# Retention and mLSTM head outputs kept with queries as rows instead of channels as rows

## The reference

```python
proj = x @ w_in[l]                 # split into r_q r_k r_v r_g, m_qk, m_v, m_o, m_i, m_f, g_a, g_b
o_ret = _head_norm(_retention(rq, rk, rv), ret_norm_g[l]) * silu(r_g)
o_ml  = _head_norm(_mlstm(mq, mk, mv, i_pre, f_pre), mlstm_norm_g[l]) * sigmoid(m_o)
mix = (sigmoid(g_a + ba) * (o_ret @ w_proj_ret[l]) + sigmoid(g_b + bb) * (o_ml @ w_proj_mlstm[l])) @ w_out[l]
x = _layer_norm(alpha * x + mix, ...);  x = _layer_norm(alpha * x + swiglu(x), ...)
```

## Time and profile before

| | before |
|---|---|
| time, median of 3 runs | 2080.57 us (2076.99 to 2081.15) |
| profiled execution, its own time | 2082.32 us |
| its span in the trace | 2080.2 us |
| PE busy in the span | 98% |
| DVE / ACT / POOL busy | 61% / 48% / 4% |
| mean granted TensorE clock | 0.993 |

### The profile page before, as it was taken

How to read it: one execution, slowest core, us unless ns; L and a number is a source line. 1 busy time by engine, 2 the same in 40 slices (tenths; PEclk the granted TensorE clock), 3 DMA queues, 4 the chain that set the end, 5 groups by cost and what they waited for, 6 DMA issues and landing times.

```text
span 2080.2 us, 37327 instructions
## 1 busy us (share of the span) xinstructions
PE 2047.2 (98%) x15913; PEld 1959.2 (94%) x15928; DVE 1271.8 (61%) x1141; ACT 999.4 (48%) x929; POOL 86.8 (4%) x58
## 2 busy tenths in 40 slices
PE   9999999999999999899999999999999999999998
PEld 8999998999999998589999999999998999999997
DVE  6556655755665576637555665676446674676545
ACT  5545645543454356435344663544344554544333
POOL 2000000100000001101000000100000000100000
PEclk9999999999999999999999999999999999999999
DMA  7555453455555544125554434464554544464552
GB/s 297 182 181 182 166 178 118 161 188 181 181 203 182 192 179 174 61 87 206 181 187 179 164 141 163 176 243 166 183 192 157 197 142 142 167 228 183 192 181 102
DMA packets 51217, 362.31 MB, mean 174 GB/s; under 512 B 5680, under 2 KB 6832, under 8 KB 7728
## 3 DMA queue, kind: packets, MB, share of 16 engines
q1 hardware_dynamic: 49856, 353.05, 47.4%
q0 software_dynamic: 1264, 7.80, 1.1%
HBM read 359.78 MB, written 1.05 MB: 173 GB/s over the span
## 4 chain that ended last, share of the span: by engine, by line
PE 92%; DVE 3%; ACT 2%; DMA 1%; issue 1%; POOL 0%; DVEq 0%; SPq 0%; ACTq 0%; POOLq 0%
PE ps L242 22%; PE ps L243 22%; PE ps L244 22%; PE ps L518 3%; PE ps L519 3%; PE ps L517 3%; PE ps L289 2%; PE ps L290 2%; PE ps L291 2%; PE ps L501 1%; PE ps L495 1%; PE ps L496 1%; DMA raw<-in_slots 1%; PE ps L789 1%; PE ps L1619 1%
## 5 line engine op out<-in xcount | busy, mean ns | idle before, releaser
L238 DVE TENSOR_TENSOR wlo<-raw,whi 128x2048 fp32r<-128x2048 f32 x325 | 758.9, 2337 | 476.4 <-ACT whi L233 475.6
L242 PE MATMUL ps<-in_hi,whi 128*128 128x256 f32 x3596 | 1016.7, 283 | 3.8 <-DVE in_lo L313 3.5
L243 PE MATMUL ps<-in_lo,whi 128*128 128x256 f32 x3596 | 1006.5, 280 | 0.0
L244 PE MATMUL ps<-in_hi,wlo 128*128 128x256 f32 x3596 | 1005.3, 280 | 0.0
L233 ACT ACTIVATE whi<-raw 128x2048 fp32r<-128x2048 f32 x325 | 619.4, 1908 | 214.8 <-PE ps L244 184.4
L242 PEld LDWEIGHTS ps<-in_hi,whi 128*128 128x128 f32 x3596 | 678.6, 189 | 12.3 <-DVE in_lo L313 4.7
L243 PEld LDWEIGHTS ps<-in_lo,whi 128*128 128x128 f32 x3596 | 678.7, 189 | 3.5 <-issue 1.7
L244 PEld LDWEIGHTS ps<-in_hi,wlo 128*128 128x128 f32 x3596 | 678.4, 189 | 0.0
L242 PE MATMUL ps<-h_hi,whi 128*128 128x256 f32 x480 | 134.5, 280 | 0.0
L243 PE MATMUL ps<-h_lo,whi 128*128 128x256 f32 x480 | 133.9, 279 | 0.0
L244 PE MATMUL ps<-h_hi,wlo 128*128 128x256 f32 x480 | 133.9, 279 | 0.0
(11 more groups left out here) (295 smaller groups left out, 2162.9 us busy)
## 6 DMA issues: line engine op xcount, KB each, us to landing
raw<-in_slots SPq DMA_DIRECT2D x333, 1024.0 KB, 4.8
ws<-in_lngb POOLq DMA_DIRECT2D x4, 1024.0 KB, 5.1
ws<-in_mem_t POOLq DMA_DIRECT2D x2, 1024.0 KB, 10.1
consts<-in_consts SPq DMA_DIRECT2D x1, 1600.0 KB, 14.6
consts<-in_consts POOLq DMA_DIRECT2D x1, 1472.0 KB, 6.7
x<-in_x_t SPq DMA_DIRECT2D x1, 1024.0 KB, 7.9
y<-x SPq DMA_DIRECT2D x1, 512.0 KB, 2.6
y<-x SPq DMA_DIRECT2D x2, 256.0 KB, 2.1
```

The source lines that it names most:

```text
L238: dve.tensor_tensor(wlo[:, j], raw[:, j], whi[:, j].bitcast(F32), ALU.subtract).then_inc(lo_ready, 1)
L242: pe.matmul(out, whi[:, j, o:o + n], hi, start=start, stop=False, skip_group_check=True)
L243: pe.matmul(out, whi[:, j, o:o + n], lo, start=False, stop=False, skip_group_check=True)
L244: return pe.matmul(out, wlo[:, j, o:o + n], hi, start=False, stop=stop, skip_group_check=True)
```

## The change

The scores are now the stationary operand and the values are streamed, so the outputs of both mixers have queries as rows and the 256 channels of a head along the free axis. `pe_values2` makes 12 products of 256 columns per mixer. Mean and variance come from DVE's BN_STATS and BN_AGGR straight from PSUM, factor and shift are 128 x 8 numbers, and ACT applies them while it copies PSUM to SBUF (`act_head_norm`, 8 activations of 256 columns). For mLSTM the sum `den` is now a one-column product behind each value product with the same stationary scores; the reciprocal is 128 x 8 numbers and is folded into factor and shift. exp(-m) is turned together with the row `a` (4 tiny products in place of 2), so that L1797's spread has only the running maximum: 256 columns in place of 512. The eight output-gate slots 17 to 24 are made in the tok form, and each gate is one DVE multiplication of 128 x 2048. The result is turned back by 16 TensorE transposes per mixer (`pe_head_turn`), for retention between slots 30 and 31, for mLSTM between slots 33 and 34. The gain of each channel is applied while the turned result is split (`act_head_hi`, `dve_head_lo`, per 256 columns from PSUM). POOL's additions, ACT's squares and all of `pe_head_sums` are gone.

```diff
         def pe_values2(pe, v, sums=None):
+            def both(t, h, w, first, done, tk):
+                last = pe.matmul(head_out(t, h), w, v[:, tk, h * 256:(h + 1) * 256], start=first, stop=done, ...)
+                if sums is not None:
+                    last = pe.matmul(sums(t, h), w, ones[:, 0:1], start=first, stop=done, skip_group_check=True)
+                return last
             for h in range(HEADS):
-                for d in range(2):
-                    o = ps[:, h, d * T:(d + 1) * T]
-                    w = slice(h * 256 + d * P, h * 256 + (d + 1) * P)
-                    pe.matmul(o, v[:, 0, w], scores2[:, h, P:384], start=True, stop=False, ...)
-                    last = pe.matmul(o[:, P:T], v[:, 1, w], scores2[:, h, 0:P], start=False, stop=True, ...)
+                both(0, h, scores2[:, h, P:2 * P], True, True, 0)
+                both(1, h, scores2[:, h, 2 * P:384], True, False, 0)
+                last = both(1, h, scores2[:, h, 0:P], False, True, 1)
...
+        def act_head_norm(act, n, out):
+            act.wait_ge(hn_shift, 2 * n + 2)
+            for t in range(2):
+                for h in range(HEADS):
+                    g = 4 * t + h
+                    last = act.activation(out[:, t, h * 256:(h + 1) * 256], head_out(t, h), ACT.Identity,
+                                          scale=hn_scale[:, g:g + 1], bias=hn_bias[:, g:g + 1])
+            last.then_inc(hn_done, 1)
...
+        def pe_head_turn(pe, n, src):
+            for k in range(DT):
+                for t in range(2):
+                    last = pe.transpose(head_turned(n, k)[:, t * P:(t + 1) * P], src[:, t, k * P:(k + 1) * P], ident)
+                if k % 4 == 3:
+                    last.then_inc(hn_turned, 1)
...
-            run(S_MQK + 1, S_MQK + 3)
-            pe_head_sums(pe, n, "mean")
-            run(S_MQK + 3, S_MV)
-            run(S_MV, S_MV + 2, True)
-            pe_head_sums(pe, n, "var")
-            run(S_MV + 2, S_RG, True)
-            pe.wait_ge(cen_act, CA("factor", n))
+            run(S_MQK + 1, S_MV)
+            run(S_MV, S_RG, True)
+            pe.wait_ge(hn_done, n + 1)
             for h in range(HEADS):
-                last = pe.matmul(ps[:, h, :], const("sel")[0:4, h * P:(h + 1) * P],
-                                 rows[0:4, ROW_M:ROW_E + 1, :].rearrange("p a b -> p (a b)"), start=True, stop=True)
+                last = pe.matmul(ps[:, h, 0:T], const("sel")[0:4, h * P:(h + 1) * P], rows[0:4, ROW_M, :],
+                                 start=True, stop=True)
...
-            run(S_RG + 3, S_MO)
+            run(S_RG + 3, S_MO + 1, True)
             pe.wait_ge(ml_dve, LD("scores", l))
-            for h in range(HEADS):
-                pe.matmul(den[:, h], ones, scores2[:, h, P:384], start=True, stop=False, skip_group_check=True)
-                last = pe.matmul(den[:, h, P:T], ones, scores2[:, h, 0:P], start=False, stop=True, ...)
-            run(S_MO, S_MO + 2)
-            pe.wait_ge(ml_dve, LD("denom", l))
-            pe_values2(pe, l_v).then_inc(ml_pe, 1)
-            run(S_MO + 2, S_GA + 3)
-            pe_head_sums(pe, n + 1, "mean")
-            run(S_GA + 3, S_GB + 2)
-            pe_head_sums(pe, n + 1, "var")
+            pe_values2(pe, l_v, lambda t, h: den[:, 4 * t + h:4 * t + h + 1]).then_inc(ml_pe, 1)
+            run(S_MO + 1, S_GA, True)
+            run(S_GA, S_GB + 2)
+            pe.wait_ge(ret_dve, TD("gated", l))
+            pe.wait_ge(hn_done, n + 2)
+            pe_head_turn(pe, n, r_o)
```

More of the change, by code:

```diff
@@ L1639, in pe_head_sums @@
-        def pe_head_sums(pe, n, step):
-            out = head_mean if step == "mean" else head_var
-            pe.wait_ge(cen_pool, CP(step, n))
-            for h in range(HEADS):
-                last = pe.matmul(out[:, h], ones, c_sq[:, 2 * h], start=True, stop=True, skip_group_check=True)
-            last.then_inc(cen_pe, 1)
-        def dve_head_centre(dve, n, src):
-            dve.wait_ge(cen_pe, CP("mean", n))
-            for h in range(HEADS):
-                v = src[:, 2 * h:2 * h + 2]
-                last = dve.scalar_tensor_tensor(v, bcast(head_mean[:, h], 2), -1.0 / 256, v, ALU.mult, ALU.add)
-            last.then_inc(cen_dve, 1)
@@ L1672, in build, with dve_head_lo @@
+        def dve_head_lo(dve, n, sp, gain, k0, m, at):
+            dve.wait_ge(split_hi, sp + 1)
+            for k in range(k0, k0 + m):
+                last = dve.scalar_tensor_tensor(in_lo[:, at + k - k0], head_turned(n, k), gain(k),
+                                                in_hi[:, at + k - k0].bitcast(F32), ALU.mult, ALU.subtract)
+            last.then_inc(split_lo, 1)
         LN_SUMS = 12
@@ L1783, in layer2_pe @@
             pe.wait_ge(ml_act, LA("en", l))
-            for t in range(2):
-                last = pe.matmul(ps[:, 7, 256 + 4 * t:260 + 4 * t], rows[0:4, ROW_A, t * P:(t + 1) * P], ident[0:4, 0:4],
-                                 start=True, stop=True, skip_group_check=True)
-            last.then_inc(ml_pe, 1)
-            run(S_MQK + 1, S_MQK + 3)
-            pe_head_sums(pe, n, "mean")
-            run(S_MQK + 3, S_MV)
-            run(S_MV, S_MV + 2, True)
-            pe_head_sums(pe, n, "var")
@@ L1793, in layer2_pe @@
-            run(S_MV + 2, S_RG, True)
-            pe.wait_ge(cen_act, CA("factor", n))
+            for i, row in enumerate((ROW_A, ROW_E)):
+                for t in range(2):
+                    o = 256 + 8 * i + 4 * t
+                    last = pe.matmul(ps[:, 7, o:o + 4], rows[0:4, row, t * P:(t + 1) * P], ident[0:4, 0:4],
+                                     start=True, stop=True, skip_group_check=True)
+            last.then_inc(ml_pe, 1)
+            run(S_MQK + 1, S_MV)
+            run(S_MV, S_RG, True)
@@ L2138, in layer2_dve @@
[L2138 to L2144 removed]
+            dve.reciprocal(l_rd[:, :], l_rd[:, :]).then_inc(ml_dve, 1)
+            dve.wait_ge(ml_dve, LD("recip", l))
```

238 lines of the change are left out of this document (121 added, 117 removed).

## The result

| | before | changed |
|---|---|---|
| median, four executions each on one chip | 2080.86 us (2076.99 to 2081.43) | 2067.86 us (2063.28 to 2070.20) |
| profiled execution, its own time / span | 2082.32 / 2080.2 us | 2063.28 / 2061.5 us |
| granted clock, mean | 0.993 | 0.997 |
| DVE / ACT / POOL busy | 61% / 48% / 4% | 60% / 48% / 3% |

The ratio is 0.9939 [0.9924, 0.9955].

The account below looks back on a forecast made before the run. PE bounds the kernel, busy 98% of the span. Per layer 14.33 us removed less 10.89 added gives 3.44, 6.9 for two; 2082.3 - 6.9 + 0.2 for waits = 2075.6 us, range 2070.5 to 2080.5.

Parts of the forecast that it names:

- (e): Result turned back on PE: 32 transposes a layer, two records each, 0.218 us a transpose, 6.98 us added.
- (c): Spread of rows over partitions: 6.83 us, half of it clock, becomes 2.0 us; gain 4.83 us a layer.
- (d): Value products on PE: 5.2 us both before and after, so nothing gained.
- (f): Twelve one-column sums a layer, 24 records at 0.117 us: 2.80 us added, bounds 0 and 3.8.
- (g): Two more products for turning exp(-m): 4 x 0.117 = 0.47 us added a layer.
- (h): Eight slots in tok form, 5.68 us for 5.60 each: 0.64 us added a layer.
- rival 2: The shortened spread still brings the half clock: 2079 to 2082 us; chance 0.10.
- Slot 16: Statistics chain ahead of this slot: 1.0 us late by upper bounds, expected 1 us early, no PE wait.
- Slot 27: lo(25) behind the mLSTM shift takes 5.7 us against PE's 5.60; 0.1 us a layer allowed, 0.2 in all.
- Rival 4: Statistics chain late, 1.5 us at slot 16 and 0.5 at slot 27 a layer: 2079.6 us; chance 0.12.
- Rival 1: One-column sums hide behind streaming, 2 x 2.8 us less: about 2070.5 us; chance 0.12.
- Rival 3: Transposes cool the clock, a 3.4 us fall behind each of four stretches: 2089 us; chance 0.06.

Follow-up runs that it names:

- turn_twice: Changed kernel with each group of 16 transposes issued twice into the same PSUM places; 2074.79 us, ratio 0.9972 to the kernel before.
- turn_as_matmul: Changed kernel with its 64 transposes made as plain float32 products with the identity; 2076.36 us, ratio 0.9982 to the kernel before.
- sums_last: Changed kernel with all twelve one-column mLSTM sums moved behind all twelve value products; 2068.35 us, ratio 0.9945 to the kernel before.
- sums_more: Changed kernel with the first of each group of one-column sums issued four times, 24 more products a layer; 2079.56 us, ratio 1.0002 to the kernel before.
- gates_w: Changed kernel with output-gate slots 17 to 24 weight-stationary again, which changes the outputs; 2066.50 us, ratio 0.9936 to the kernel before.
- fewer_sums: Changed kernel with eight one-column sums for twelve (DVE adds two score blocks first) and rows turned by transposes; 2064.46 us, ratio 0.9919 to the kernel before.
- spread_512: Changed kernel with the spread made over both rows again, 512 columns, second half unused; 2075.02 us, ratio 0.9974 to the kernel before.
- after_again: The changed kernel measured again, unaltered, on the same chip as turn_as_matmul and fewer_sums_again; 2068.84 us, ratio 0.9940 to the kernel before.
- before_split: Kernel before with its 512-column spread cut into four products of 256 columns ahead of slot 16 and four behind; 2081.91 us, ratio 1.0008.
- fewer_sums_again: The kernel fewer_sums measured again, on the same chip as the changed kernel's repeat; 2065.51 us, ratio 0.9929 to the kernel before.

## Why the prediction was wrong, step by step

**The step that failed is (e): "32 transposes. Each is two records."** A transpose is one record. By starts the sixteen take 1.67 us, 3.34 a layer and not 6.98, which is 7.3 us too much in the sum for two layers. I had carried the x2 of the plain float32 products (L1609, L1619, L1643) over to an operation that is called MATMUL in the trace as well. The distance between two records, 0.108, was right; the count was wrong. It was there to be read: L1643 stands in the program as four products a call and in the trace as x8, but L469 of the earlier trace rows stands in the program as eight transposes (two halves of four) and in the trace as x8. I multiplied by two records where the row had one for each transpose. turn_twice measures the price and turn_as_matmul the error. The Trainium skill ("TensorE: Matmul & The Clock Gate", section "Terms") says that the transpose mode is four times as fast for FP32; it points to the right side, but here 0.107 against 0.218 us is a factor of two.

The other steps, per layer:

| step | predicted us | measured us | from |
|---|---|---|---|
| (c) spread, full clock | 2.0 | 1.92, 2.0 with the matmul behind | starts above |
| (d) value products | 5.2 | 5.18 | sums_last |
| (e) transposes | 6.98 | 3.34 | starts above |
| (f) twelve sums | 2.80 | 7.78 - 5.18 = 2.60 | starts above; sums_more |
| (g) two more row turns | 0.47 | 1.05 - 0.60 = 0.45 | L1821, |
| (h) tok form | 0.64 | 0.33, 0.61 | gates_w |

Net of the clock the prediction had 0.04 us gained a layer: 6.88 + 2.62 + (6.83 - 3.4 - 2.0) for what goes, 10.89 for what comes. With the measured costs, 7.03 (with step (h) left at 0.64), it is 3.9 a layer. The distances show 4.5 and 4.6. The 0.6 to 0.7 left over are no step of mine.

In all, the forecast of the gain was 8.0 us short. Step (e) is 7.3 of it, steps (f) and (g) and the wait that was not paid 0.6, and 1.3 are left over without a step; against that the clock gave about 1.1 less than forecast. Two sums of the prediction are off as well: DVE's statistics at slot 16 end at 10.8 and not 10.6, and rival 2 starts at 2075.6 + 1.7 = 2077.3 and not 2079. Neither touches the forecast.

**The clock.** Step (c) gave 3.4 us a layer. Both falls of before (6.83 us each) are missing in the changed kernel's first profile, as forecast, but that was partly luck: the argument, from one row over 16 partitions, does not reach so far. Over nine profiles of kernels with the short spread in the changed kernel's place (the changed kernel twice, turn_twice, turn_as_matmul, fewer_sums twice, sums_last, sums_more, gates_w) a fall of 3.41 us stands behind 5 of 18 spreads; behind the long one it stood 4 times of 4, 6.83 us in before and 3.41 in spread_512. So rival 2 is partly right: the fall still comes in some executions, and costs 1.7 when it does. The medians fit that: 13.0 less 9.1 of work leaves 3.9 for the clock in the first comparison, and beside after_again 11.0 less 9.1 leaves 1.9, against about 5 in the forecast (6.8 less the 1.75 that it took off for its base).

**Waits.** Slot 16: expected 1 us early, `lo(14)` ends at 1217.76 and the slot begins a tok slot ahead of the spread, at 1224.93 - 5.68 = 1219.25, so 1.5 early; BN_AGGR over six numbers takes 0.08 us and BN_STATS out of PSUM 0.34, both under the bound. Slot 27: 0.1 allowed; the step between two starts at 1294.07 is 0.18 instead of 0.12, so under 0.1. Rival 4 did not occur.

**Rival 1** gave 2070.5 for a mechanism that sums_more refutes. That the time came out nearer to it than to my case is no support for it. **Rival 3** is refuted by turn_twice. There the Trainium skill ("TensorE: Matmul & The Clock Gate", section "Part 4: PE-mode transpose"), by which transposes do not count as activity in the same way and the full clock does not engage for them, disagrees with the traces: the clock is 1.00 in and behind 3.41 us of nothing but transposes in turn_twice, and in the earlier trace rows it rose to 1.00 behind 3.3 us of them.

## What to carry to other kernels

Before a count of records from one kind of instruction prices another, set the count in the program beside the count in the trace for that very kind; here one row with both would have been worth 7 us. A float32 turn cost half as much in the transpose form as in a product with the identity, and a small float32 product cost about 0.22 us with 128 columns, with 4 and with 1, so where PE is the limit it pays to add operands first on an engine that has time. Compare such kernels from one landmark of PE to the next, less half of the time at the lower clock: that repeated to 0.2 us or better where the whole times of two profiles were 6.6 apart.

## What I had not expected of the hardware

- The granted clock fell to 0.50 (1.2 GHz) while PE was busy all the time, behind products over 4 partitions that lasted only 1.92 us (5 of 18 times, and 2 of 4 in before_split) and once behind twelve one-column products in a row. What decides whether it falls stays open; fewer_sums_again and fewer_sums are the same program and differ in it.
- In the kernel before, the slots behind mLSTM's value products ran slightly slower. In PE's timeline of before, from the start of slot 23 to the head sums behind slot 27:

```profile
1281.61 0.37 PE L242 MATMUL ps<-in_hi,whi 128*128 128x256 f32 x1
...
1309.96 1.89 PE L1643 MATMUL ps<-ws,consts 128*128 128x256 f32 x8
```

  and of the changed kernel, the start of slot 23 and then that of slot 25, from which I count up to the first transpose at 1316.54:

```profile
1271.51 0.28 PE L290 MATMUL ps<-whi,in_hi 128*128 128x256 f32 x1
...
1282.87 0.28 PE L243 MATMUL ps<-in_hi,whi 128*128 128x256 f32 x1
```

  240 matmuls in 28.35 us (0.1181 each) against 288 in 33.67 (0.1169). Over the slots of a layer that can make up the 0.6 us left over above, and it lies from that place on: from the start of slot 23 to the turn at the end of layer one before took 1408.74 - 1281.61 = 127.13 us and the changed kernel 1398.05 - 1271.51 = 126.54, 0.59 less, where the prices (3.34 of transposes for 3.44 of sums, 0.16 for two tok slots) ask for 0.06 more. gates_w shows the slower step in its layer one and not in its layer two, so it isn't bound to one program; its cause stays open and no experiment tried it by itself.
- The time that the first block spends at clock 0.50 varies between profiles of kernels that share this block, 10.2 to 20.5 us. By half of the difference, an estimate, that alone moves a whole time by up to 5 us. The changed kernel's first profiled execution, 4.6 under its median, has 10.2 there; its second, 1.1 over its median, has 20.5. It is not all that varies there: sums_more has the same 10.2 and still enters layer one 2.9 us later than the changed kernel (1122.55 against 1119.66).
